# The experts' rows summed in PSUM onto x's turned rows, x's memory lent to the expert weights, and the next block's halves taken straight from the banks

## The reference, cut to what matters

```
first block
  x  = x + merged @ w_out                      # three gated branches (pool, MLA, memory attention)
  h2 = rms_norm(x, ffn_norm_g)
  x  = x + moe(h2)                             # 32 experts in 4 groups, top 2 of the chosen group, d_expert 256
  x  = rms_norm(x, final_norm_g)               # "fin"
second block
  h  = rms_norm(x, g_pre_mix)                  # "pre"
  m  = chunk_relpos_attention(h, w_qkv, w_o)   # 16 heads of 64
  x  = x + rms_norm(m, g_post_mix)
  x  = x + rms_norm(swiglu(rms_norm(x, g_pre_ffn), w_gate, w_up, w_down), g_post_ffn)
```

## Time and profile before

| | us |
|---|---|
| median of three runs | 805.26 |
| the profiled execution's own time | 804.51 |
| its span, first to last instruction | 802.7 |
| TensorE busy (matmul), share of the span | 740.9, 92% |
| VectorE / ScalarE / GpSimd busy | 420.4 / 329.5 / 33.5 |
| DMA | 203.95 MB, mean 254 GB/s |

### The profile page before, as it was taken

One profiled execution on the slowest core, in us unless ns is written; L12 is line 12 of the kernel. 1 busy time (PEld: TensorE's weight loads), 2 busy tenths in 40 slices (PEclk: granted clock), 3 DMA queues, 4 the chain that ended last, 5 costly groups with the idle time before them and its releaser, 6 DMA issues.

```text
span 802.7 us, 12226 instructions
## 1 busy us (share of the span) xinstructions
PE 740.9 (92%) x5046; PEld 598.1 (75%) x5046; DVE 420.4 (52%) x739; ACT 329.5 (41%) x583; POOL 33.5 (4%) x65
## 2 busy tenths in 40 slices
PE   8999899999999999997776768999998999999996
PEld 7899698888788875553443437989877788888885
DVE  4647646666767521110100108666657777677665
ACT  5666465555444421110110115556546443444442
POOL 0700000000000000000000003000002000000000
PEclk9999999999999999998988989999999999999999
DMA  9764476556978979999999999944333465465201
GB/s 320 261 205 137 142 277 223 171 169 212 363 259 319 345 319 422 420 421 420 420 422 421 421 392 351 373 178 150 128 135 124 139 218 201 158 210 163 100 1 53
DMA packets 83849, 203.95 MB, mean 254 GB/s; under 512 B 6992, under 2 KB 47824, under 8 KB 71248
## 3 DMA queue, kind: packets, MB, share of 16 engines
q1 hardware_dynamic: 83792, 203.15, 68.4%
HBM read 202.09 MB, written 1.05 MB: 253 GB/s over the span
## 4 chain that ended last, share of the span: by engine, by line
PE 77%; DMA 13%; DVE 4%; ACT 4%; issue 1%; SPq 1%; POOL 0%; DVEq 0%; ACTq 0%
PE ps L608 40%; PE ps L676 10%; DMA ext<-in_w_gate_e 7%; PE ps L928 6%; PE ps L679 5%; DMA big<-in_w_up_e 3%; PE ps L962 2%; PE ps L949 2%; PE ps L907 2%; DMA big<-in_rel_ext 1%; DVE wl L1513 1%; ACT junk L1148 1%; PE ps L571 1%; SPq L455 1%; ACT wh L1139 1%
## 5 line engine op out<-in xcount | busy, mean ns | idle before, releaser
L1513 DVE TENSOR_TENSOR wl<-raw,wh 128x1024 fp32r<-128x1024 f32 (+3 forms) x180 | 213.0, 1200 | 130.7 <-ACT wh L1139 129.0
L1139 ACT CAST wh<-raw 128x1024 fp32r<-128x1024 f32 (+3 forms) x180 | 181.8, 1029 | 69.5 <-PE ps L608 48.2
L608 PE MATMUL ps<-wh,fra 128*128 128x512 f32 (+3 forms) x668 | 189.1, 368 | 0.4 <-DVE gb L1725 0.4
L608 PEld LDWEIGHTS ps<-wh,fra 128*128 128x128 f32 x668 | 118.7, 189 | 18.8 <-DVE wl L1513 0.8
L608 PE MATMUL ps<-wl,fra 128*128 128x512 f32 (+3 forms) x334 | 121.4, 363 | 0.0
L676 PE MATMUL ps<-fra,wh 128*128 128x512 f32 x352 | 110.9, 396 | 1.4 <-DVE S L2032 1.3
L608 PE MATMUL ps<-fra,wh 128*128 128x256 f32 x464 | 87.0, 289 | 2.8 <-DVE fra L1941 2.6
L679 PEld LDWEIGHTS ps<-fra,wl 128*128 128x128 f32 x352 | 66.1, 188 | 15.5
L608 PEld LDWEIGHTS ps<-fra,wh 128*128 128x128 f32 x464 | 73.4, 195 | 4.3 <-DVE fra L1941 2.9
L928 PE MATMUL ps<-ext,big 128*32 128x256 f32 x480 | 53.5, 443 | 22.6 <-DMA ext<-in_w_up_e 10.7
L608 PE MATMUL ps<-wh,frb 128*128 128x512 f32 x240 | 74.3, 391 | 0.0
(11 more groups left out here) (244 smaller groups left out, 913.6 us busy)
## 6 DMA issues: line engine op xcount, KB each, us to landing
ext<-in_w_up_e SPq DMA_DIRECT2D x23, 1024.0 KB, 26.6
raw<-in_w_in SPq DMA_DIRECT2D x16, 1024.0 KB, 5.1
raw<-in_w_gate_e SPq DMA_DIRECT2D x16, 1024.0 KB, 9.1
raw<-in_w_down_e SPq DMA_DIRECT2D x16, 1024.0 KB, 27.3
raw<-in_w_qkv SPq DMA_DIRECT2D x12, 1024.0 KB, 12.6
raw<-in_w_gate SPq DMA_DIRECT2D x11, 1024.0 KB, 5.4
raw<-in_w_up SPq DMA_DIRECT2D x11, 1024.0 KB, 5.1
raw<-in_w_down SPq DMA_DIRECT2D x11, 1024.0 KB, 4.9
```

The costliest lines, as they stand in the source:

```text
L608: t = e.matmul(o, a, w, start=first and n == 0, stop=final and n == 2, skip_group_check=not check)
L1139: e.copy(halves(q)[0], piece_view(q)).then_inc(*up("wh", q))
L1513: e.tensor_tensor(l, piece_view(q), h.bitcast(F), ALU.subtract).then_inc(*up("wl", q))
```

## The change

1. **Combine turned.** x's turned rows stay in banks 4 to 7, two blocks of 128 features in a bank (`turned(k)`), and `combine` adds onto them: eight products of 256 columns a group, with `YE` stationary and `CM` moving. `x1T` is copied out of the banks in four pieces, three by VectorE and the last by ScalarE.
2. **X as 24th slot.** X is not needed after h2, so it becomes a slot of the ring. Unit 23 goes there as soon as h2 is written. Near the end two pairs of units swap slots, so that the slots under the halves come free early.
3. **Halves from the banks.** After the last combine ScalarE makes the high half straight from a bank with the gain as its scale (eight of 128x256), and VectorE the low half (eight more). The four additions of X, the transposes to banks 0 to 3 and the separate multiplications by the gain are gone. The banks are copied to `MOT` (two copies on each of the two engines), and TensorE turns them back for the norms inside `quarter(0)`, eight transposes after each of q's pieces. Fin's squares (four of 512 columns), its roots and block 1's output (four of 512 columns) now read those banks.
4. **Spread later.** The spread of `krow` and the keeping of q and k come after all six pieces; one piece of the next quarter goes ahead of the first attention step, so the whole filling is one piece earlier.
5. **Count earlier.** The two products of the count follow the rank in the router, into bank 0, and VectorE derives from them a factor, 0 or 1, on the combine weights.
6. **Latents' banks.** The key latents turn in banks 4 and 5 instead of 6 and 7, VectorE rotates the keys one step earlier, and the two rotated query tiles swap banks 6 and 7.
7. **Gate summed early.** The gate sum is split from the scaling and comes right after the gate's weight stream, in step 0 too.
8. Names of semaphores are merged, and the path for an overfull expert, not taken here, is adapted.

```diff
-                + [(RAW + EXT, None)])
+                + [(RAW + EXT, None), (RAW + EXT + BIG + 1, None)])
+        for n, m in ((-14, -4), (-13, -3)):
+            order[n], order[m] = order[m], order[n]
...
+            if n == 23:
+                e.wait_ge(*at("h2", 1))
...
-            enter(6, "lo", "lat2", 0, 1)
+            enter(4, "lo", "lat2", 0, 1)
...
-            enter(7, "kr")
+            enter(5, "kr")
...
-                enter(6 + i, "kept", "qr", i)
+                enter(7 - i, "kept", "qr", i)
...
+        def turn_x1(a, i):
+            for k in range(a, a + 4):
+                if i == 0 and k % 2 == 0:
+                    enter(4 + k // 2, copied(4 + k // 2), 4 + k // 2)
+                if k == a:
+                    e.wait_ge(*at("x1", a // 4, i))
+                t = e.matmul(turned(k)[:, P * i:P * i + P], X[:, i, P * k:P * k + P], ident, start=(i == 0 and k % 2 == 0),
+                             stop=False, is_transpose=True, skip_group_check=True)
+            t.then_inc(*up("turn", "x1", a, i))
...
+        enter(0, "counted")
+        e.matmul(bank[0][:, 64:96], ones, M[:, 0, :], start=True, stop=False)
+        e.matmul(bank[0][:, 64:96], ones, M[:, 1, :], start=False, stop=True).then_inc(*up("count"))
...
-            for c in range(2):
-                e.wait_ge(*at(("YE act", "YE dve")[c], g))
-                for i in range(2):
-                    b = 4 + 2 * i + c
-                    if g == 0:
-                        enter(b, "MO", i, c)
-                    t = e.matmul(bank[b][:, :], CM[:, P * i:P * i + P], YE[c], start=(g == 0), stop=(g == 7))
+            for k in range(8):
+                if k % 4 == 0:
+                    e.wait_ge(*at(("YE act", "YE dve")[k // 4], g))
+                t = e.matmul(turned(k), YE[k // 4][:, P * (k % 4):P * (k % 4) + P], CM, start=False, stop=(g == 7),
+                             skip_group_check=True)
...
-        for c in range(2):
-            turn("pre", MO, 8, (2 * c, 2 * c + 1), [[at("MO", i, c)] for i in range(2)], freed="gained", only=(4 * c,))
+        def turn_back(h):
+            for i in range(2):
+                enter(4 + 2 * h + i, "block 1", h, i)
+                for b in (4 + 2 * h, 5 + 2 * h):
+                    e.wait_ge(*at(copied(b), b))
+                for j in range(4):
+                    k = 4 * h + j
+                    t = e.transpose(bank[4 + 2 * h + i][:, P * j:P * j + P], MOT[:, 256 * k + P * i:256 * k + P * i + P],
+                                    ident)
+                t.then_inc(*up("turned back", h, i))
...
         for n, _ in enumerate(quarter(0)):
-            if n == 4:
-                spread("krow", 6)
+            if n < 2:
+                turn_back(n)
+        spread("krow", 6)
         fill = other_quarters()
+        next(fill)
...
-        split_to(LATE + 1)
-        high_rows(0)
+        split_to(LATE)
+        for k in range(8):
+            e.wait_ge(*at("combined", 7, k | 1))
+            e.activation(hT[0][:, k, :], turned(k), ACT.Copy, scale=G[:, G_MIX2 + k:G_MIX2 + k + 1]).then_inc(
+                *up("hi", "pre", k))
+        split_to(LATE + 1)
+        for b in (4, 5):
+            e.wait_ge(*at("lo", "pre", 2 * (b - 4) + 1))
+            e.copy(MOT[:, 512 * (b - 4):512 * (b - 4) + 512], bank[b][:, :]).then_inc(*up("MOT act", b))
         split_to(LATE + 2)
-        high_rows(4)
+        for h in range(2):
+            for i in range(2):
+                e.wait_ge(*at("turned back", h, i))
+                if h or i:
+                    e.wait_ge(*own())
+                square(rms("fin")[0][:, 2 * h + i:2 * h + i + 1], bank[4 + 2 * h + i][:, :], junk, "fin", h, i)
+            split_to(LATE + 3 + h)
...
+            e.wait_ge(*at("count"))
+            e.tensor_reduce(tm_[:, 0, :], bank[0][:, 64:96], AX, ALU.max).then_inc(*routed())
+            e.wait_ge(*own())
+            e.tensor_scalar(tm_[:, 1, :], tm_[:, 0, :], float(limit), None, ALU.is_le).then_inc(*routed())
+            e.tensor_copy(flag[:, :], tm_[:, 0, :]).then_inc(*up("counted"))
+            e.wait_ge(*own())
+            e.tensor_scalar(kept_W, W, tm_[:, 1, :], None, ALU.mult).then_inc(*routed())
...
+        split_to(LATE)
+        for k in range(8):
+            e.wait_ge(*at("hi", "pre", k | 1))
+            e.scalar_tensor_tensor(hT[1][:, k, :], turned(k), G[:, G_MIX2 + k:G_MIX2 + k + 1], hT[0][:, k, :].bitcast(F),
+                                   ALU.mult, ALU.subtract).then_inc(*up("lo", "pre", k))
+        split_to(LATE + 1)
+        for b in (6, 7):
+            e.wait_ge(*own())
+            e.tensor_copy(MOT[:, 512 * (b - 4):512 * (b - 4) + 512], bank[b][:, :]).then_inc(*up("MOT dve", b))
...
-        vals = stream(("v", 0))
-        next(vals)
+        whole(stream(("v", 0)))
         spread_row("krow", 6)
         keep_q(0)
         keep_k(0)
-        whole(vals)
...
                 whole(stream(("fg", c)))
+                summed_gate(c)
```

More of the change, by code:

```diff
@@ L158, in plan @@
                 + [(RAW + z, None) for z in (6, 7)] + left[1:] + near + [(RAW + z, None) for z in (4, 5)] + far
-                + [(RAW + EXT, None)])
[L160 to L164, removed]
+                + [(RAW + EXT, None), (RAW + EXT + BIG + 1, None)])
+        order = [ring[n % len(ring)][0] for n in range(self.expert_end - self.dense_end)]
+        held = dict(ring)
+        for n, m in ((-14, -4), (-13, -3)):
+            order[n], order[m] = order[m], order[n]
+        for u, z in zip(range(self.dense_end, self.expert_end), order):
+            self.slot.append(z)
+            self.before.append(held[z])
+            held[z] = u
         left = [u for u in range(self.expert_end - len(ring), self.expert_end) if self.slot[u] < RAW]
@@ L433, in rows_at, with turned, copied @@
         return bank[b][:, 256 * half_:256 * half_ + 256]
+    def turned(k):
+        return bank[4 + k // 2][:, 256 * (k % 2):256 * (k % 2) + 256]
+    def copied(b):
+        return "MOT act" if b < 6 else "MOT dve"
     def causal_parts(s):
@@ L983, in tensor @@
                 general_tensor(e)
[L986 to L987 removed]
+        def turn_back(h):
[8 more added lines that the diff above has]
+                t.then_inc(*up("turned back", h, i))
         def quarter(c):
[L991 to L992 removed]
+            yield from features(("q", c), 0, hT, ("kept q", c), row=("lo", "pre") if c == 0 else None)
             yield from features(("k", c), 1, hT, ("kept k", c))
@@ L1121, in general_tensor @@
         e.wait_ge(f_done, 2)
+        for k in range(8):
+            for i in range(2):
+                t = e.transpose(turned(k)[:, P * i:P * i + P], MO[:, i, P * k:P * k + P], ident)
+        t.then_inc(f_back, 1)
     def scalar(e, real):
@@ L2107, in gpsimd @@
         e.memset(gb[:, 0, 0:P], 0.0).then_inc(*up("zeroed"))
-        e.memset(half, -0.5).then_inc(*up("half"))
+        e.memset(half, -0.5).then_inc(*up("pool step", "half"))
         e.wait_ge(*have("gvec"))
@@ L2147, in gpsimd @@
         root("h2", 0, 1024, 2, more=True)
-        for i in range(2):
-            e.wait_ge(*at("squared", "fin", i))
-            root("fin", i, 1024)
+        e.wait_ge(*at("squared", "fin", 1, 1))
+        root("fin", 0, 1024, 2, more=True)
         for i in range(2):
```

192 lines of the change are left out of this document (89 added, 103 removed).

## The result

| | before | after |
|---|---|---|
| median of the runs, us | 805.27 (4 runs, 804.41 to 807.41) | 794.84 (4 runs, 794.3 to 795.8) |
| span of the profiled execution | 802.7 | 793.6 |

The account below looks back on a forecast made before the run. TensorE was taken to bound the dense stretches and the DMA queues the experts. Terms -3.0 + 0 - 2.5 - 2.0 - 1.3 = -8.8 from 804.51 gave 795.7, forecast as a median of 796.5, range 792 to 801.

Parts of the forecast that it names:

- Latents' banks: Latents, TensorE: three waits of 0.9, 0.9 and 1.2 us go, -3.0; bounds 0 to -3.0.
- Router: Router: a 0.35 us wait closes, the count's two products add about 0.4 us; net 0, bounds -0.4 to +0.8.
- The 24th slot: DMA-bound expert stage: one more unit loads in the DMA's pause, -2.5 us; bounds 0 and -2.5.
- Between the blocks: Last combine to first scores: q starts 4.5 us earlier, new waits of 1.0 and 1.8 follow; -1.5.
- The further 0.5: Scores at 528.76: their 0.50 us wait for kept k goes as the filling is a piece ahead, -0.5.
- Feed-forward: Feed-forward: the 1.33 us wait goes as the gate sum comes earlier, -1.3; bounds 0 and -1.3.
- The page on VectorE and GpSimd: Passage between the blocks: VectorE subtractions of two SBUF tiles exclude GpSimd's SBUF reads; GpSimd's three steps would take 4.2.
- the low price: Passage between the blocks: GpSimd's three steps priced near the quick root's 0.55, 2 us in all.
- The new gaps: Rival, passage between the blocks: gaps of 1.0 and 1.8 slow the clock, costing 1.6 us, 798.1; chance 0.12.
- No stall at all: Rival, passage between the blocks: block 1's chain is quicker and TensorE keeps its 4.3 us, 793.7; chance 0.15.
- Slot without gain: Rival, expert stage: the 24th slot gives nothing, 799.0, chance 0.10; with early waits replaced too, 802.0, chance 0.05.
- slower: Rival, passage: TensorE stays at half clock after the two gaps, up to 815.5 us; chance 0.03.

Follow-up runs that it names:

- e8_norot: Kernel after with VectorE's last key rotation back at its old place, one step later: 798.0 against 805.13, ratio 0.9915.
- e2_noslot: Kernel after without the 24th slot and without the swapped pairs of slots: 798.9 against 805.73, ratio 0.9913.
- e3_gate: Kernel before with only the feed-forward's gate sum taken ahead: 804.4 against 805.73, ratio 0.9972.
- e1_latents: Kernel before with only the Latents' banks changed and the last key rotation issued earlier: 801.94 against 805.73, ratio 0.996.
- e4_warm: Kernel before with eleven unread filler products on TensorE in the idle 2.65 us between the blocks: 805.56 against 805.73, ratio 0.9998.
- e5_ahead: Kernel after with one piece's high half on ScalarE taken ahead of the pre norm's squares: 797.51 against 805.13, ratio 0.9904.
- e9_passage: Kernel after with Latents' banks, rotation, 24th slot and gate sum put back, leaving the passage between the blocks: 803.54 against 805.72, ratio 0.9972.
- e6_row: e5_ahead's kernel with the last piece's low half on VectorE put behind the row of key scales and kept q and k: 794.92 against 805.13, ratio 0.9869.
- e7_noswap: Kernel after with the 24th slot but without the swap of two pairs of slots: 795.98 against 805.13, ratio 0.9887.

## Why the prediction was right, point by point

**Latents' banks: right in kind, the size off by a quarter.** Forecast -3.0, the three idle times of the earlier trace rows; measured -3.71. A wait costs more than the idle time its row shows, and I priced the waits by these rows alone. Three waits cost 0.24 more each; e8_norot gives one of them singly, 1.08 for 0.9. Where the rest lies is read best at the feed-forward. In the earlier trace rows the two products behind the wait take 1.00, in after 0.70: 0.30 lie in slower first products. From the start of the spread to the start of these products it is 2.02 in before (621.87 to 623.89) and 0.43 in after (614.63 to 615.06), 1.59 less for an idle time of 1.33, because without the wait the product starts 0.25 before the spread's 0.68 are over. Together 1.89, against 1.90 measured. The wait of 1.2 at the Latents shows the same overlap: 1.39 less from start to start.

**Router:** net 0 forecast, -0.14 measured.

**The 24th slot: right.** -2.5 forecast, -2.64 from before to after and 2.45 undone in e2_noslot, in the experts' column alone. The combine's doubled loads of stationary blocks cost nothing: 3.72 us for its eight products (sixteen records), 3.70 for the four of before (eight records).

**Between the blocks: the total right, one support of it not.** The chain came out as laid. Moved onto the old trace's clock (5.39 us later) v's second piece came at 501.7, forecast 501.6; kept q was ready at 506.5, forecast 506.7; the first scores ended at 510.6, forecast 510.5. TensorE waited 0.71 and 1.37 where the forecast had 1.0 and 1.8, and GpSimd's three steps took 1.24 from start to end and not 2; VectorE was idle beside all but their last 0.35. A piece was priced at 2.85, where the row named for it gives 2.81; it takes about 2.9 in both kernels, and nothing hangs on this. E to F gained 1.41, forecast 1.5. But 0.83 of it is the fall of the clock behind the old gap, which e3_gate did not have, so the passage gives 0.6 in some executions and 1.4 in others. I had priced the clock at 1.5 to 1.7 by work lost at half rate; e3_gate shows 0.83. The 1.5 was counted down from a trace in which the clock had fallen, and it is luck in part that it was met: against an execution like e3_gate's the same chain gains 0.6.

**The further 0.5** of the scores' wait at 528.76 came, 0.44, but my reason (the filling a piece ahead) isn't what the runs show: e1_latents has the old filling and lost the wait as well. In before VectorE's first softmax step waits for GpSimd's memset, which waits for the bias table:

```profile
510.99 0.29 DVE L1585 CUSTOM_DVE_ANT_0 S<-ps,big 128x128 f32<-128x128 f32 x1 [2.64 <-POOL big L2157]
```

The table took 10.8 us to land there and 9.9 in e1_latents, where that wait of VectorE is 1.7. The later the memset ends, the longer TensorE's wait: it ends 2.62 us after the start of the first scores in before, 2.63 in e3_gate and 2.76 in e4_warm, where that wait is 0.50, 0.52 and 0.65, and 1.70 in e1_latents, where there is none. In after the table is issued 11.0 us ahead of the scores instead of 9.2, the memset ends 0.79 after their start, and VectorE waits for the scores. That the late softmax made kept k late is read from the order on VectorE; no run isolates it.

**Feed-forward: right in kind, undersized.** Forecast -1.3, measured -1.90 (e3_gate alone -1.88), the same error as at the Latents: 1.33 idle and 0.57 around it, taken apart above.

**The page on VectorE and GpSimd.** The Trainium skill, "SBUF — State Buffer", section "Who interferes with whom", has a VectorE instruction with two inputs in SBUF and a GpSimd instruction that reads SBUF exclude each other for a whole instruction. In after the first three steps ran into one only at their end, the next four met none, and the low price held; the sum behind them met one and took 1.26, where e5_ahead has 0.20 for it. In e5_ahead two of the four met one and took 1.23 and 1.62 for 0.19 and 0.56. Rule and runs agree.

**The rivals.** The new gaps did not slow the clock in any of the nine traces with waits of 1.33 to 1.38 before the next q; in e5_ahead, where that wait was 2.02, they did, and E to F lengthened as that rival said. No stall at all: refuted by the two waits. Slot without gain and slower: refuted.

All in all -8.8 were forecast and -10.4 measured; the missing 1.6 are 0.7 at the Latents, 0.6 at the feed-forward and 0.3 spread over the small columns.

## What to carry to other kernels

Price a wait that goes at its idle time plus what the first instructions behind it and the lost overlap with the one ahead of it cost, here 0.2 to 0.6 us each. Where TensorE and another engine wait for each other in turn, moving one of them alone gives little or nothing, and the wait that grows can cost clock as well: move both, and look at which wait grows. Measure tenths by cutting the timelines at equal work, since start-up and clock move the whole time by more.

## What was unexpected of the hardware

The clock's fall is a matter of the execution, not of the code alone: behind the 2.65 us gap it came in two traces of three, behind the feed-forward's 1.33 us wait in one of four (before, e1_latents and e9_passage without, e4_warm with), and at the router's filler products in three (e6_row, e7_noswap, e8_norot), with TensorE not idle there, for 1.34 to 1.37 us from B to C. The page "TensorE: Matmul & The Clock Gate", section "What's actually happening", of the Trainium skill calls the low rate the default that activity lifts. That TensorE was slowed while its products were small and followed one another does not speak against it, and no run here shows what decides between two executions of equal code.
